# Moving the block sums of twelve modulation tiles from TensorE to VectorE in a two-layer diffusion block

## The reference, cut to what matters

```
def adaln(cond, w_mod, b_mod):
    return jnp.split(jax.nn.silu(cond) @ w_mod + b_mod, 6, axis=-1)
...
for l in range(DEPTH):
    sh1, sc1, g1, sh2, sc2, g2 = adaln(c, w_mod[l], b_mod[l])
    csh1, csc1, cg1, csh2, csc2, cg2 = adaln(c_ctx, w_mod[l], b_mod[l])
    ... token mixer (Fourier and state-space branches), then channel mixer
def swiglu(t, w_gate, w_up, w_down):
    return (jax.nn.silu(t @ w_gate) * (t @ w_up)) @ w_down
```

## Time and profile before

| | |
|---|---|
| median of 3 runs | 2102.3 us |
| span of the profiled execution, from its first to its last instruction | 2109.0 us |
| TensorE matmul busy in the span | 2035.3 us (97%) |
| VectorE busy | 1399.7 us (66%) |
| ScalarE busy | 940.9 us (45%) |
| mean granted TensorE clock | 0.978 |
| DMA, mean | 251 GB/s |

### The profile page before, as it was taken

How to read it: one execution, slowest core, us unless ns; L and a number is a source line. 1 busy time by engine, 2 the same in 40 slices (tenths; PEclk the granted TensorE clock), 3 DMA queues, 4 the chain that set the end, 5 groups by cost and what they waited for, 6 DMA issues and landing times.

```text
span 2109.0 us, 24695 instructions
## 1 busy us (share of the span) xinstructions
PE 2035.3 (97%) x10138; PEld 1539.4 (73%) x10138; DVE 1399.7 (66%) x1873; ACT 940.9 (45%) x859; POOL 0.2 (0%) x4
## 2 busy tenths in 40 slices
PE   5999899999999999999989999999999999999997
PEld 2456364447777777788887888888888888888886
DVE  5675536662222323646268898888988889898986
ACT  2212112121221221321227777777777777676775
POOL 0000000000000000000000000000000000000000
PEclk8999999989999999999989999999999999999998
DMA  9432694332435431368528999899998999999994
GB/s 401 84 133 107 199 247 183 140 109 95 184 140 219 160 150 70 120 200 200 180 120 317 373 353 371 340 364 369 360 371 332 369 360 363 359 346 369 360 364 158
DMA packets 83841, 529.30 MB, mean 251 GB/s; under 512 B 23056, under 2 KB 49552, under 8 KB 52752
## 3 DMA queue, kind: packets, MB, share of 16 engines
q1 hardware_dynamic: 62976, 508.65, 65.5%
q10 hardware_dynamic: 20752, 19.05, 2.6%
HBM read 509.39 MB, written 18.28 MB: 250 GB/s over the span
## 4 chain that ended last, share of the span: by engine, by line
PE 90%; DVE 4%; DMA 3%; ACT 1%; issue 1%; SPq 0%; DVEq 0%; ACTq 0%
PE ps L1692 19%; PE ps L2121 14%; PE ps L2106 14%; PE ps L2107 14%; PE ps L1701 6%; PE ps L1705 6%; PE ps L1708 6%; PE ps L1635 2%; PE ps L1926 1%; DMA GR<-in_w_mod 1%; PE ps L2052 1%; DVE WL L1517 1%; DMA mring<-in_moe_down 1%; PE ps L2035 1%; PE ps L1934 1%
## 5 line engine op out<-in xcount | busy, mean ns | idle before, releaser
L1517 DVE TENSOR_TENSOR WL<-mring,WH 128x2048 fp32r<-128x2048 f32 x336 | 755.2, 2287 | 108.2 <-ACT WH L949 108.0
L949 ACT ACTIVATE WH<-mring 128x2048 fp32r<-128x2048 f32 x336 | 626.1, 1913 | 139.2 <-PE ps L2121 117.4
L2106 PE MATMUL ps<-WH,XGh 128*128 128x512 f32 x896 | 355.9, 397 | 2.4 <-ACT WH L949 2.4
L2107 PE MATMUL ps<-WH,XGl 128*128 128x512 f32 x896 | 351.5, 392 | 0.0
L2121 PE MATMUL ps<-WL,XGh 128*128 128x512 f32 x896 | 221.7, 390 | 0.0
L1311 DVE TENSOR_TENSOR ringl<-ring,FWH 128x4096 fp32r<-128x4096 f32 (+2 forms) x21 | 82.3, 3917 | 187.6 <-ACT FWH L794 187.6
L1692 PE MATMUL ps<-aT,ring 128*128 128x512 f32 (+1 forms) x576 | 199.8, 507 | 0.0
L2106 PEld LDWEIGHTS ps<-WH,XGh 128*128 128x128 f32 x896 | 169.3, 189 | 36.7 <-issue 2.5
L794 ACT ACTIVATE FWH<-ring 128x4096 fp32r<-128x4096 f32 (+2 forms) x21 | 67.8, 3231 | 285.4 <-DMA ring<-in_ffn_gu 152.9
L2107 PEld LDWEIGHTS ps<-WH,XGl 128*128 128x128 f32 x896 | 169.5, 189 | 33.9
L2121 PEld LDWEIGHTS ps<-WL,XGh 128*128 128x128 f32 x896 | 168.2, 188 | 34.9
(11 more groups left out here) (291 smaller groups left out, 2234.6 us busy)
## 6 DMA issues: line engine op xcount, KB each, us to landing
mring<-in_moe_gate SPq DMA_DIRECT2D x56, 2048.0 KB, 9.6
mring<-in_moe_up SPq DMA_DIRECT2D x56, 2048.0 KB, 9.6
mring<-in_moe_down SPq DMA_DIRECT2D x56, 2048.0 KB, 9.5
ring<-in_w_mod SPq DMA_DIRECT2D x23, 2048.0 KB, 8.1
ring<-in_w_in SPq DMA_DIRECT2D x11, 2048.0 KB, 10.4
ring<-in_ffn_gu SPq DMA_DIRECT2D x11, 2048.0 KB, 10.9
cks<-CW ACTq DMA_DIRECT2D x16, 512.0 KB, 3.1
ring<-cks SPq DMA_DIRECT2D x4, 2048.0 KB, 12.2
```

Of the source, the lines that this page charges most:

```text
L949: nc.scalar.activation(WH[buf][:, o], mring[t % MRING][:, o], ACT.Copy).then_inc(high_done, 1)
L1517: V.tensor_tensor(WL[buf][:, o], mring[t % MRING][:, o], WH[buf][:, o].bitcast(F32), ALU.subtract).then_inc(low_done, 1)
L2106: mm(out_, ah, WH[buf][:, o:o + 512], start=(first and q == 0), stop=False)
L2107: mm(out_, al, WH[buf][:, o:o + 512], start=False, stop=False)
```

## The change

Layer 1's twelve modulation tiles are no longer summed by `mod_sums`. VectorE multiplies each block of 512 columns by the SiLU of its input channel, which is a value for each partition, and adds it to a running sum in `acc`, one for each condition: 16 instructions for a tile, 8 behind each of the two blocks of the weight tile (`mod_add`). TensorE then sums over the partitions only, with one column of ones (`pick`), for two tiles at once (`mod_pair`), behind the first block of the next weight tile. A ring slot that held a modulation tile is free when VectorE has read it. The modulation tiles now go with the weight tiles 1 to 5, 7, and 9 to 14, and not with 1 to 12. The low part of the last hidden block is written ahead of the weights' low part as before, and now also ahead of `mod_add`.

```
+MOD_TILE = (1, 2, 3, 4, 5, 7, 9, 10, 11, 12, 13, 14)
+        pick = sb(top, "pick", [P, 15])
+        acc = sb(ffn, "acc", [P, 3, 2, 512])
...
         for i, key in enumerate(ffn_tiles):
-            stream += [key] + (mods(FFN_MOD + i - 1) if 0 < i <= ADA_TILES - FFN_MOD else [])
+            stream += [key] + (mods(FFN_MOD + MOD_TILE.index(i)) if i in MOD_TILE else [])
... (SyncE, ring_load)
-                    if before[0] == "mod":
+                    if before[0] == "mod" and before[2] >= FFN_MOD:
+                        sp.wait_ge(mod_step, 2 * KD * (before[2] - FFN_MOD + 1))
+                    elif before[0] == "mod":
                         sp.wait_ge(mod_rows_done, before[2] + 1)
... (ScalarE; the same edit in the loop of the down tiles)
-                                if 3 <= ahead < ADA_TILES - FFN_MOD + 3:
-                                    mod_rows(FFN_MOD + ahead - 3)
+                                if ahead - 3 in MOD_TILE:
+                                    mod_rows(FFN_MOD + MOD_TILE.index(ahead - 3))
... (VectorE)
+            link(V.memset(pick[:], 0.0))
+            link(V.memset(pick[:, 7:8], 1.0))
...
+            def mod_add(i, half):
+                if i not in MOD_TILE:
+                    return
+                t = FFN_MOD + MOD_TILE.index(i)
+                n = stream_at[("mod", 0, t)]
+                wv_ = ring[n % RING][:].rearrange("p (k c) -> p k c", k=KD)
+                if half == 0:
+                    dve.wait_ge(landed[n % RING], 16 * (n // RING + 1))
+                    if t >= FFN_MOD + 3:
+                        dve.wait_ge(mod_rows_done, (t - 3) // 2 * 2 + 2)
+                done = 2 * KD * (t - FFN_MOD)
+                for k in range(4 * half, 4 * half + 4):
+                    for v in range(2):
+                        sum_ = acc[:, t % 3, v, :]
+                        if k == 0:
+                            ins = V.tensor_scalar(sum_, wv_[:, k, :], silu4[:, k, 0, v:v + 1], None, ALU.mult)
+                        else:
+                            dve.wait_ge(mod_step, done + 2 * k + v - 1)
+                            ins = V.scalar_tensor_tensor(sum_, wv_[:, k, :], silu4[:, k, 0, v:v + 1], sum_,
+                                                         ALU.mult, ALU.add)
+                        ins.then_inc(mod_step, 1)
...
                             if m > m0:
                                 hidden_low(m - 1, m0)
+                            if m % 2 and m == m0 + size - 1:
+                                hidden_low(m, m0)
+                            mod_add(ahead - 2, m % 2)
                             if m % 2:
-                                if m == m0 + size - 1:
-                                    hidden_low(m, m0)
                                 weights_low(ahead)
                                 ahead += 1
                         for m in range(8):
                             residual(("down" + str(part), l, m), l, m, 40, 0, part == 1)
+                            mod_add(ahead - 2, m % 2)
... (TensorE)
+            def mod_pair(t):
+                if t % 2 == 0:
+                    return
+                pe.wait_ge(mod_step, 2 * KD * (t - FFN_MOD + 1))
+                pe.wait_ge(mod_rows_taken, t // 4)
+                for i in (t - 1, t):
+                    for v in range(2):
+                        g, r = 32 * (2 * (i % 2) + v), 2 * (i % 4) + v
+                        last = mm(ps[g:g + 8, 2, :], pick[:, 7 - r:15 - r], acc[:, i % 3, v, :],
+                                  start=(i % 4 < 2), stop=(i % 4 >= 2), skip_group_check=True)
+                last.then_inc(mod_rows_done, 2)
... (behind block m of weight tile i_, gate-and-up and down tiles alike)
+                                if m == 0 and i_ - 1 in MOD_TILE:
+                                    mod_pair(FFN_MOD + MOD_TILE.index(i_ - 1))
... (at the end of weight tile i_)
-                        if 1 < i_ <= ADA_TILES - FFN_MOD + 1:
-                            mod_turn(FFN_MOD + i_ - 2)
-                        if 0 < i_ <= ADA_TILES - FFN_MOD:
-                            mod_sums(FFN_MOD + i_ - 1)
+                        if i_ - 2 in MOD_TILE:
+                            mod_turn(FFN_MOD + MOD_TILE.index(i_ - 2))
```

More of the change, by code:

```diff
@@ L152, in program @@
         mod_rows_done = sem("mod_rows_done")
+        mod_step = sem("mod_step")
         mod_rows_taken = sem("mod_rows_taken")
```

## The result

| | before | after |
|---|---|---|
| median of the runs | 2102.1 us (4 runs) | 2141.5 us (4 runs, 2138.7 to 2150.7) |
| ratio, with 95% interval | | 1.0192 [1.0175, 1.0209] |
| the pair measured again | 2105.0 us (23 runs) | 2137.3 us (6 runs), 1.0169 [1.0142, 1.0196] |
| span of the profiled execution | 2109.0 us | 2139.9 us |

The change makes the kernel 39.4 us slower in the first measurement and 32.3 in the second; forecast were 34.2. From here on the stage means the stretch of TensorE from the first gate product, 464.19 us before and 464.09 after, to the first sum of squares behind the last down tile, 870.57 before and 904.06 after. It takes 406.4 us before (406.4 again in a second profile) and 440.0 after (439.6 in a second): 33.6 us more.

What follows compares the result with a forecast made beforehand. TensorE bounds the kernel before; after, a loop of 28.7 us a tile through VectorE and the ring slot takes over. Second down start 32.1 us late, with last pair and turn 34.2 us, on 2102.3: 2136.5 us, range 2116 to 2154.

Steps and rivals of the forecast that it cites:

- TensorE's saving: Layer 1's twelve modulation tiles: sums removed save 24.2 us, six pairs cost 7.0 us, net gain 17.2 us.
- Price of VectorE's instruction: A scalar_tensor_tensor of 512 columns costs 0.665 us, the two tensor_scalar 0.40 each; 10.1 us a tile.
- The rival without overlap: Each VectorE instruction costs its full 0.743 us, 12 us more in all: 2148 us; chance 9 in 100.
- The loop: Weight load, high part, low part (16.2 us) and VectorE's work (12.5 us) follow without overlap: 28.7 us a tile.
- E(1): E(i) is when VectorE ends the second half of tile i, and weight tile i+2's load can be issued; E(1) 525.4.
- Down starts: Down products of the two parts start at 632.0, 13.5 us late, and at 846.2, 32.1 us late.
- the middle: From first down start to tile 10: 67.7 us, one pair replacing four sums; tile 10 then 8.4 us late.
- The clock: Slow clock behind TensorE's wait adds 1.8 us at the first down tile; the second starts as slow as before.
- The rival of a long low clock: Each big stall is followed by some 10 us at half speed, 5 us instead of 1.8: 2145; chance 8 in 100.
- Sum: Second down start 32.1 us late, with the last pair and turn behind it 34.2 us: 2136.5 us.
- What the profile was to show: VectorE in SyncE's waits, low parts 28 to 29 us apart, TensorE waiting 8 and 11 us at down starts.
- The rule that speaks for the change: VectorE's low share: its work fits and TensorE's 17.2 us stay, 2085; chance 6 in 100, 3 more near break-even.

Runs made afterwards that it cites:

- noslot: Changed kernel with VectorE's 192 instructions reading a constant table, the twelve modulation tiles not loaded and no load waiting for one: 2088.2 us, ratio 0.9943 to before.
- reorder: Changed kernel with all 16 VectorE instructions of a modulation tile placed directly ahead of the weights' low part: 2086.8 us, ratio 0.9942 to before.
- half: Changed kernel with VectorE leaving out the odd blocks, 8 of its 16 instructions of a modulation tile: 2090.0 us, ratio 0.9948 to before.
- half_ahead: Changed kernel with the last tile's second half and this tile's first half both ahead of the weights' low part: 2096.1 us, ratio 0.9952 to before.
- kwise: On top of reorder, the first down product of each part waits block by block for the hidden: 2091.0 us, ratio 0.9926 to before; again 2081.9.
- pe_sums: Changed kernel with TensorE summing as before and VectorE summing nothing, modulation tiles kept in their new places: 2104.6 us, ratio 0.9997 to before.

## Why the prediction was right

It named 2136 us and a range of 2116 to 2154; the medians are 2141.5 and 2137.3. Step by step:

- *TensorE's saving.* 17.2 us net. noslot and reorder show it where VectorE stays out of the way: 14.9 and 15.1 less stage. The 2.2 that are missing are no single thing. A turn and a sum stood ahead of the first down start and covered a wait for the last hidden block. TensorE before:

```profile
616.72 1.90 PE L1635 MATMUL ps<-ring,silu 128*8 128x512 f32 x16
```

With them gone TensorE waits 2.28 us there, and the 12 matmuls behind take 4.57 us in place of 3.06: 3.8 us lost. At the second down start the same wait is followed by ten matmuls in 2.56 us in place of 4.07: 1.5 back, which the prediction had not counted on. A pair was put at 1.16 us and takes 1.04 (0.97 from start to start); the 1.71 and 0.3 us that it was built from stand in no row, and the runs show only the whole.
- *Price of VectorE's instruction.* Put together from shorter shapes: 0.665 us from start to start. Measured: eight take 5.38 us; less one duration of 0.743 and by seven that is 0.662. The two tensor_scalar take 0.79, 0.40 each as taken. The rival without overlap falls. By the Trainium skill ("VectorE: DVE Perf Modes", section "The DRAIN you can't avoid") a next operation does not start until the pipe is empty, but one that is not held starts earlier. The trace agrees with the second half: each instruction starts 0.08 us ahead of the end that the profile shows for the one in front.
- *The loop.* E(1) to E(4) were 525.4, 554.1, 582.8 and 611.4; the issues behind them are at 524.23, 552.84, 582.01 and 610.57, with the whole stream 1.2 us ahead of the kernel before at tile 2 already, where the slow stretch that begins the stage ended sooner; the forecast had no term for this, and it is luck that it more than covers the one load that came late. Periods 28.6, 29.2 and 28.6 against 28.7; the 29.2 has a load 0.6 us longer. E(9) was 713.1 and E(10) 741.2; the issues behind them are at 712.23 and 740.08. This is the step on which all stood, and half (23.4) and half_ahead (23.9) confirm its formula at two other amounts of work.
- *Down starts.* 632.1 and 846.2 forecast; 631.28 and 844.84 measured, 12.8 and 30.9 late. Between them the middle took 69.2 us to tile 10 (700.49) for the 69.5 of 1.8 + 67.7.
- *The clock.* Put at 1.8 us for the first down start, and at nothing more for the second, which was slow before as well. The first takes 4.49 us for 12 matmuls instead of 3.06, 1.4 more with a clock of 0.65; the second 4.61 for 10, where it took 4.07 before, 0.5 more. The rival of a long low clock falls. The slow 8 us behind 594 (clock 0.60) lie inside the loop's slack, as assumed.
- *Sum.* Parts of the stage: 12.8 + 18.1 + 2.7 = 33.6, for 13.5 + 18.6 + 2.1 = 34.2.
- *What the profile was to show.* VectorE's line in the queue's waits, low parts 28 to 29 us apart and 11 to 12 us of idle ahead of each are there. TensorE's wait at the first down start was put at 8 us and is 6.7; at the second 11 and 12.4. At the pairs, put at 4 to 6, they are 1.96, 2.19, 1.05 and one 4.19, and two have none: the forecast was too high, as TensorE also waits at high parts (5.89 at 594.24, ahead of the pair with 2.19) and at a turn (4.55 at 780.90).

What the stage doesn't explain: the first measurement has 5.8 us more than 33.6, the second 1.3 less. That the first lies 5.2 us above the forecast and the second 1.9 below is within what the stretches outside vary by; the stage is what bears the forecast out. The stretches outside are the same code and vary between executions of one kernel, below; which of them made the first difference was not settled.

The rule that speaks for the change, VectorE 27% busy beside a full TensorE, gave 2085. It is near the time of reorder (2086.8): right about amounts, and the order made the difference.

## What to carry to other kernels

An engine that works in order and stands idle ahead of one instruction has that idle time to give only to work placed directly ahead of this instruction. For new work ask what it is queued ahead of, and which load its ring slot lets go. If the load of a tile waits for work that stands ahead of the use of that same tile, load, conversion and work add up to one period (here 16.2 + 12.5 us against 22.9), and the busy shares show nothing of it. Put the work where the engine waits already, just ahead of the waiting instruction; here that turned 1.017 to 1.019 into 0.994.

## What the runs showed of the hardware that was not expected

The same length of wait of TensorE was followed by the slow clock at one place and not at another. Two starts of down products in reorder, TensorE in order of time:

```profile
607.08 4.57 PE L1749 MATMUL ps<-hidh,FWH 128*128 128x512 f32 x12 [2.28 <-issue]
...
793.37 2.56 PE L1749 MATMUL ps<-hidh,FWH 128*128 128x512 f32 x10 [2.28 <-issue]
```

And the stretches behind them, columns as in rows 2:

```profile
607.00:612.00 5.00, 4.92 (x15) 3.92 (x16) 0.00 (x0) 0.66 (x1) 0.00 (x0) 0.66 0.98 416
793.00:798.00 5.00, 4.63 (x20) 3.86 (x21) 0.27 (x1) 1.43 (x1) 0.00 (x0) 1.00 0.99 420
```

Both waits are 2.28 us; behind the first the granted clock is 0.66, partly at the 1.2 GHz level, behind the second full. In half_ahead 3.02 us of waiting are followed by 12 matmuls in 3.00 us. The Trainium skill ("TensorE: Matmul & The Clock Gate", section "HAM oscillation — how this bites in real kernels") tells of a kernel in which waits between bursts bring the slow clock back each time. The down starts agree in part: none that had no wait ahead of it was slow (3.06 us for 12 matmuls before, 2.90 in kwise), but a wait of this size does not bring it each time. What decides was not found.

Chance ahead of the stage: the stretch from the start of the span to the first gate product, which the edits leave as it is but for two memsets of `pick`, ends at 459.1 us (reorder, noslot), 464.2 (before), 471.6 (pe_sums) or 476.3 (half_ahead). A part of it is TensorE's clock from 220 to 260 us, before and then reorder:

```profile
220.00:260.00 40.00, 35.08 (x144) 15.51 (x144) 23.59 (x63) 4.46 (x11) 0.00 (x0) 0.87 0.64 217
```

```profile
220.00:260.00 40.00, 37.20 (x168) 16.07 (x161) 24.09 (x63) 4.95 (x12) 0.00 (x0) 0.96 0.77 227
```

A total over several executions therefore hides a change of 4 us in the stage (pe_sums), and the stage read from the profile shows it.
